# Moving the scatter of the previous expert's rows from among the gate products to the head of the turn

## What is computed

```python
def moe(xn, w_router, w_gate, w_up, w_down):
    logits = (xn @ w_router).astype(jnp.float32)
    top_val, top_idx = lax.top_k(logits, TOP_K)
    top_w = jax.nn.softmax(top_val, axis=-1)
    gates = jnp.sum(jax.nn.one_hot(top_idx, N_EXPERTS, dtype=jnp.float32) * top_w[..., None], axis=-2)

    def per_seq(args):
        xs, gs = args
        hg = jnp.einsum('sd,edf->sef', xs, w_gate)
        hu = jnp.einsum('sd,edf->sef', xs, w_up)
        hh = jax.nn.silu(hg) * hu * gs[..., None].astype(xs.dtype)
        return jnp.einsum('sef,efd->sd', hh, w_down)
```

## Time and profile before

| | us |
|---|---|
| median of 3 runs | 1219.54 |
| lowest, highest | 1219.3, 1220.47 |
| the profiled execution | 1220.87 |
| its span, first to last instruction | 1218.9 |

### The profile page before, as it was taken

The page is one execution under the profiler, slowest core; times in us unless marked ns, Lnnn a source line. Parts: engine busy times, 40 slices in busy tenths (PEclk is TensorE's granted clock), DMA queues, the critical chain, the costliest instruction groups (busy, mean ns, idle before and its releaser), DMA issues.

```text
span 1218.9 us, 21799 instructions
## 1 busy us (share of the span) xinstructions
PE 1168.8 (96%) x9463; PEld 588.4 (48%) x9464; DVE 338.7 (28%) x729; ACT 212.7 (17%) x399; POOL 34.8 (3%) x65
## 2 busy tenths in 40 slices
PE   7999999999999999899899999899999889999987
PEld 4878777778765534233233433333343233334323
DVE  3666566666372302101002011010201101020112
ACT  2454333333263100000010010101010010101001
POOL 2130000000200000000000000000000000000000
PEclk9999999999999999899899999999999999999998
DMA  9614645247535899999999999999999999999993
GB/s 339 243 69 163 230 160 187 90 138 257 219 122 241 362 425 404 422 426 426 425 426 425 412 422 427 424 425 427 424 427 425 425 426 427 425 424 411 427 424 164
DMA packets 56042, 413.40 MB, mean 339 GB/s; under 512 B 4702, under 2 KB 10076, under 8 KB 32140
## 3 DMA queue, kind: packets, MB, share of 16 engines
q1 hardware_dynamic: 54464, 410.40, 82.1%
q0 software_dynamic: 944, 1.29, 0.3%
q10 hardware_dynamic: 540, 0.29, 0.1%
HBM read 410.91 MB, written 1.05 MB: 338 GB/s over the span
## 4 chain that ended last, share of the span: by engine, by line
PE 82%; DMA 9%; DVE 4%; issue 2%; ACT 2%; ACTq 0%; POOL 0%; DVEq 0%; POOLq 0%; SPq 0%
PE ps L1579 35%; PE ps L1554 6%; PE ps L1620 6%; DMA ring<-in_moe_w_gate 5%; DMA ring<-in_moe_w_down 4%; PE ps L1266 4%; PE ps L1262 4%; PE ps L1263 4%; PE ps L1558 3%; PE ps L1595 3%; PE ps L1438 2%; PE ps L1545 2%; PE ps L1389 2%; PE ps L1125 2%; ACT w_hi L918 1%
## 5 line engine op out<-in xcount | busy, mean ns | idle before, releaser
L1579 PE MATMUL ps<-ring,arena 128*32 128x448 f32 x4736 | 461.4, 548 | 12.1 <-issue 7.5
L1579 PEld LDWEIGHTS ps<-ring,arena 128*32 128x32 f32 x4736 | 155.5, 111 | 310.5 <-issue 306.5
L1620 PE MATMUL ps<-ring,arena 128*64 128x512 f32 x280 | 125.5, 602 | 14.7 <-DMA ring<-in_moe_w_down 10.7
L1621 PE MATMUL ps<-ring,arena 128*64 128x512 f32 x280 | 125.5, 602 | 0.0
L2122 DVE TENSOR_TENSOR arena<-arena,ps 128x448 f32<-128x448 f32 x38 | 22.3, 603 | 285.5 <-PE ps L1579 285.2
L1554 PE MATMUL ps<-ring,arena 128*32 128x512 f32 x504 | 87.0, 593 | 2.4 <-DVE arena L2127 2.4
L1868 DVE TENSOR_TENSOR w_lo<-ring,w_hi 128x2048 fp32r<-128x2048 f32 x31 | 71.1, 2292 | 57.1 <-ACT w_hi L918 55.1
L1555 PE MATMUL ps<-ring,arena 128*32 128x512 f32 x168 | 85.9, 593 | 0.0
L1620 PEld LDWEIGHTS ps<-ring,arena 128*64 128x64 f32 x280 | 37.3, 138 | 96.0 <-issue 71.4
L918 ACT CAST w_hi<-ring 128x2048 fp32r<-128x2048 f32 x31 | 59.1, 1909 | 112.6 <-PE ps L1266 112.6
L2104 DVE TENSOR_TENSOR h<-h,ps 128x512 f32<-128x512 f32 x32 | 22.0, 688 | 174.2 <-PE ps L1595 174.2
(11 more groups left out here) (317 smaller groups left out, 1196.9 us busy)
## 6 DMA issues: line engine op xcount, KB each, us to landing
ring<-in_moe_w_gate SPq DMA_DIRECT2D x63, 1792.0 KB, 18.9
ring<-in_moe_w_up SPq DMA_DIRECT2D x61, 1792.0 KB, 18.3
ring<-in_moe_w_down SPq DMA_DIRECT2D x56, 1792.0 KB, 21.2
ring<-in_moe_w_down SPq DMA_DIRECT2D x16, 896.0 KB, 21.3
ring<-in_ffn_w_gate SPq DMA_DIRECT2D x5, 2048.0 KB, 7.8
ring<-in_ffn_w_up SPq DMA_DIRECT2D x5, 2048.0 KB, 7.8
ring<-in_ffn_w_down SPq DMA_DIRECT2D x5, 2048.0 KB, 8.1
ring<-in_mla_w_o SPq DMA_DIRECT2D x2, 2048.0 KB, 25.1
```

Of the source, the lines that this page charges most:

```text
L1579: mm = pe.matmul(ps[Q * q:Q * q + Q, bank_of(a, j), 0:CH], lhs, w[:, c0:c0 + CH], start=first, stop=last)
L1620: pe.matmul(ps[0:NARROW, DOWN_BANK, :], lhs, w[:, 0:512], start=first, stop=last)
L1621: mm = pe.matmul(ps[64:64 + NARROW, DOWN_BANK + 1, :], lhs, w[:, 512:1024], start=first, stop=last)
```

## The change

In turns 1 to 7 the two calls of `scatter` stand ahead of the first gate row, one behind the other, where they stood behind gate rows 2 and 4. In turn 0 they stay where they were. It applies to both the narrow and the wide form, since both are made by `pe_item`.

```diff
@@ -1638,12 +1638,13 @@
             items = found[0]
 
             def pe_item(i, narrow, first):
+                if not first:
+                    scatter(i, 0)
+                    scatter(i, 1)
                 for k in range(KD):
                     products(i, "g", k, narrow, first)
-                    if k == 2:
-                        scatter(i, 0, nothing=first)
-                    if k == 4:
-                        scatter(i, 1, nothing=first)
+                    if first and k in (2, 4):
+                        scatter(i, (k - 2) // 2, nothing=True)
                 for k in range(KD):
                     products(i, "u", k, narrow, first)
                     if k == 2:
```

## The result

The changed kernel takes 1221.28 us (median of 18 runs, 1219.24 to 1223.39) against 1219.06 us for the kernel before in the same sessions (18 runs, 1217.56 to 1221.16). The ratio is 1.0017 with a 95% interval of 1.0010 to 1.0023. So the change costs 2.1 us by the ratio (1.2 to 2.8), or 2.2 by the medians, clear of zero, and lies inside the 0.2% within which I had called it the same. The forecast was 1221.9, from a kernel before at 1219.54.

What follows compares the result with a forecast made beforehand. The weight stream was taken to bound the kernel: 2.4 us (1.8 to 2.9) lost at turn 1, nothing at other heads, added to 1219.54, gave 1221.9 us. The range was 1219.0 to 1224.5.

Steps and rivals of the forecast that it cites:

- The bound and the end: Whole kernel: the weight stream at 422 to 427 GB/s sets the pace; landings later by x move the end by x.
- Price of the block: Heads of turns 1 to 7: four scatter products ahead of gate row 0 take 3.86 us, waits on adds nearly hidden.
- Head of turn 1: First up piece issued at 504.4, lead falls from 5.0 to 1.1 us, costing 2.4 us.
- The line between leads: Turn 1's loss read off a straight line from none at lead 5.0 to 2.9 us at 0.8, giving 2.7 at 1.1.
- GB/s taken for loss: Turn 1: 398 GB/s from 500 to 504, 6% under 425, counted as 0.25 us already lost.
- Head of turn 3: TensorE newly idles 1.4 us, up piece issued at 712.4, lead 4.7 us; charged nothing (0 to 0.2 us).
- Is the loss kept?: After turn 1 the stream hardly stands idle, so the 2.4 us lost there stay to the end.
- The other heads: Turns 2, 4 and 6, after narrow items: the queue is deep, so the block costs the stream nothing; value nothing.
- Nothing happens: Rival, 1219.5 us, chance 0.20: block runs inside turn 1's "issue" idle time, or a lead of 1.1 us does no harm.
- The lower clock at turn 3: Rival, 1223.3 us, chance 0.20: 1.4 us of new idle time lowers the clock, lead falls to 3.0, 1.4 us more lost.
- a dip at 712: Sign in GB/s behind turn 3's head: none was forecast; one would mean the clock fell and the prediction was wrong.
- That TensorE is the bound: Rival, 1215.1 us, chance 0.06: TensorE sets the time, so filling idle heads saves 4.4 us.

Runs made afterwards that it cites:

- the wait only: Kernel before with only the two waits for the copied down result at the head, scatter products still behind gate rows 2 and 4; 1219.2 us, ratio 0.9999.
- the longer block: Changed kernel with four more products, on constants with results overwritten, ahead of the block in narrow turns; 1227.68 us, ratio 1.0072 to the kernel before.
- four products on constants: Kernel before with four 128 x 512 products on constants, results overwritten, ahead of gate row 0 in narrow turns; 1223.95 us, ratio 1.0035.

## Why the prediction was right, and where it was off

*The bound and the end.* Right. The stream sets the pace, the end moves with the landing of one down piece, and 3 us saved on TensorE at turn 4 bought nothing.

*Price of the block.* Right: 3.79 us from the block's start to the gate rows' at turn 4 (788.93 to 792.72 with the block in wide turns, read in its timeline), against 3.86. With about equal stretches of lower clock (0.78 and 0.79, 0.75 and 0.83) it also delays the piece as said: 502.5 in the change, 498.6 with the block in wide turns only, 3.9 apart:

```profile
498.60 11.41 SPq L719 DMA_DIRECT2D ring<-in_moe_w_up  x4
```

*Head of turn 1.* The mechanism was right, the size of two terms was not. I put the issue at 504.4 by adding to 500.53, a time which itself held a long stretch of lower clock. In the profiled execution of the change that stretch was half as long (0.78 and 0.79 of the clock, not 0.66 and 0.50), so that from the block's start to the issue it took 8.6 us and not 9.9; and the block started 0.6 us earlier, at 493.95 and not 494.50. So the issue came at 502.5. The piece ahead landed 0.8 us earlier than assumed too, at 504.6, and the lead was 2.1 and not 1.1. The loss was 1.7 and not 2.4. This stretch varies from one execution to the next: over 492 to 504 us the clock's missing share adds up to 3.4 us (a mean of 0.72) in two of the twelve profiled executions (the kernel before and the wait only) and to 1.7 (0.86) in the other ten. That the stretch follows the idle time was right; its length was read from one execution and taken for a constant.

*The line between leads.* I drew it straight from no loss at 5.0 to 2.9 at 0.8. The runs show a knee near 3: from 2.9 up the step of the first piece held back stays within 0.3 us of 4.3, where the line has 1.4 lost at 3.0, and below that it rises at least one for one. The time to landing accounts for the knee. A piece with little or nothing ahead takes 7.3 us, of which 4.3 are its own bytes, so it must be issued 3.0 us ahead of the landing before it; its step is then 7.3 us less the lead. At leads of -1.4 and 0.1 the time to landing is 7.3 both times. But at 2.1 to 2.3 in turn 1 it is 7.9 to 8.6, so the steps are 0.6 to 1.3 us longer than this rule gives, and no run tells why. Here is the luck in the number: at the real lead of 2.1 the rule of the lone piece gives a loss of 0.9 us, and without 0.8 us more that no run explains the 2.4 would have been 1.5 too high.

*GB/s taken for loss.* The 0.25 us that the sum takes off as lost already, for 398 GB/s from 500 to 504, is not in the landings: the step there is 4.3. At turn 3 of the change 273 GB/s went with a step of 4.3 as well. A dip in GB/s is not a loss by itself; the loss is read from the landings.

*Head of turn 3.* The issue time was right to 0.1 us (712.34 for 712.4) and so was the idle time (1.30 for 1.4). The landing ahead came at 715.5 and not 717.1, half because less was lost at turn 1 and half because this execution's stream was 0.8 us earlier, so the lead was 3.2 and not 4.7. Even so the charge of nothing stands for the held-back piece, whose step was 4.3. Up to 0.5 us, the long step two pieces behind, is neither shown nor excluded.

*Is the loss kept?* Yes. In the block-in-narrow-turns kernel nothing is lost at turn 3, and still the median span is 2.2 us longer. In the profiled executions the stretch from the landing ahead of turn 1's first up piece to the last landing of all is 699.4 to 699.9 us in the three kernels with a lead of 2.1 to 2.3, 697.3 to 698.3 in the eight executions with a lead of 4.0 or more, and 704.5 with the longer block.

*The other heads.* Right, by the kernel with the block in wide turns.

*The rivals.* "Nothing happens" falls: the block does not run inside the idle time for "issue"; it starts after 3.63 us of it. (What TensorE does in that time no view names; that it is a fetch was my guess.) The lower clock at turn 3 falls too: 1.30 us of idle time left it at 1.00. The sign that I gave for it, a dip at 712, did show, 273 GB/s where I had said that none would follow, but with the clock at 1.00 and a lead of 3.2 us. So a dip could not tell the two apart; the granted clock could. That TensorE is the bound falls with the wide turns. The 2.0 us that the Trainium skill (DMA: Bandwidth & Descriptors, Anatomy of one DMA) states for the fixed part of a transfer, there for transfers issued by GpSimd while these are SyncE's, gave a loss of 0.9 us at the lead I assumed. This case does not agree: the lone pieces here need 3.0 us beside their bytes, and the loss was larger though the lead was longer.

*The sum.* 1.7 us at turn 1 in the profiled execution's landings, 2.1 by the ratio and 2.2 by the medians, for 2.4. The forecast in microseconds, 1221.9 for 1221.28, is also 0.5 us high because the kernel before came out at 1219.06 over 18 runs and not at the 1219.54 of three.

## What to carry to other kernels

Where a stream of transfers sets the time, cost a reordering on the compute engine by what it does to the lead: from the issue of the transfer that it holds back to the landing of the one ahead. While the lead stays above the time of a lone transfer less its own bytes (3.0 us here) a delay is free; below it each microsecond is paid at least in full, and here it never came back, so look for the one or two places where the queue is short, here the first turns after start-up and after a slow item. Read the loss from the landings and not from GB/s, and compare a long step with those at long leads first. And read a stretch of lower clock from several executions before building an absolute time on it.

## What the runs showed of the hardware

The four products on constants in narrow turns left the span 2.0 us longer but added 2.8 us outside it, between the span and the measured time (median 4.78 us against 1.95; 8 of 10 runs above 4). With the block ahead of gate row 0 as well it was 3.52. No other kernel here had a median above 2.01. So two times may differ by something that no view of the profile shows, and it is worth comparing spans beside times.

At turn 2 the idle time for "issue" ahead of the first wide body grew from 3.77 us before to 5.72 in the changed kernel, while the first product behind it started at the same time (583.07 before, 583.17 after), although TensorE had come to the head 1.9 us earlier. It does not hang on the block at the head of wide turns: it was 5.88 us with the block in narrow turns only and 4.52 with it in wide turns only, and 3.65 and 3.46 in the kernels with the wait alone and with the products on constants. It cost nothing that could be seen, as the queue was 20 us deep, and its cause is open.
